# Where the running sum of the experts gets its scaled residual, and which places hold the weights of the second pair

## What is computed

```python
def grouped_moe(h, router_w, router_bias, w_gate, w_up, w_down):
    ...
    a = jnp.einsum('td,edf->etf', t, w_gate)
    u = jnp.einsum('td,edf->etf', t, w_up)
    hidden = jax.nn.silu(a) * u * gates.T.astype(t.dtype)[..., None]
    out = jnp.einsum('etf,efd->td', hidden, w_down)
    ...
    for l in range(DEPTH):
        ...
        x = layer_norm(ALPHA * x + mix, ln1_g[l], ln1_b[l])
        ffn = grouped_moe(x, router_w, router_bias, w_gate[l], w_up[l], w_down[l])
        x = layer_norm(ALPHA * x + ffn, ln2_g[l], ln2_b[l])
```

## Time and profile before

| | us |
|---|---|
| median of 3 runs | 1938.81 (1935.81 to 1940.58) |
| the profiled execution | 1934.94 |
| its span on the core | 1933.2 |
| TensorE busy | 1876.1 (97%) |
| DVE busy | 775.4 (40%) |
| DMA moved | 539.60 MB, mean 279 GB/s |

### The profile page before, as it was taken

How to read it: one execution, slowest core, us unless ns; L and a number is a source line. 1 busy time by engine, 2 the same in 40 slices (tenths; PEclk the granted TensorE clock), 3 DMA queues, 4 the chain that set the end, 5 groups by cost and what they waited for, 6 DMA issues and landing times.

```text
span 1933.2 us, 30131 instructions
## 1 busy us (share of the span) xinstructions
PE 1876.1 (97%) x12621; PEld 1218.6 (63%) x12621; DVE 775.4 (40%) x1463; ACT 298.1 (15%) x609; POOL 401.0 (21%) x406
## 2 busy tenths in 40 slices
PE   8999999999999999999999999999999999999996
PEld 7999988656644444444389989886565444444442
DVE  5657546643502111011486655566424021111015
ACT  1104210110211101111111141210102111111111
POOL 4467671012000000000005667710220000000001
PEclk9999999999999999999999999999999999999999
DMA  7444442228999999999944434421399999999997
GB/s 250 154 131 132 148 158 67 88 70 347 372 406 399 421 425 414 429 428 423 393 152 155 141 122 153 153 67 67 102 382 367 412 411 421 426 417 428 429 422 282
DMA packets 124649, 539.60 MB, mean 279 GB/s; under 512 B 14704, under 2 KB 19312, under 8 KB 85360
## 3 DMA queue, kind: packets, MB, share of 16 engines
q1 hardware_dynamic: 124528, 537.86, 71.2%
HBM read 535.73 MB, written 2.10 MB: 278 GB/s over the span
## 4 chain that ended last, share of the span: by engine, by line
PE 85%; DVE 8%; DMA 5%; issue 1%; ACT 1%; SPq 0%; DVEq 0%; ACTq 0%
PE bank L1539 20%; PE bank L1000 14%; PE bank L1005 10%; PE bank L1584 9%; PE bank L942 7%; PE bank L1425 6%; PE bank L1036 3%; DMA region_b<-in_w_up_dram 3%; PE bank L1276 3%; DMA x_t<-in_w_down_dram 2%; PE bank L1481 2%; PE bank L886 1%; PE bank L1437 1%; PE bank L1439 1%; DVE bank L2139 1%
## 5 line engine op out<-in xcount | busy, mean ns | idle before, releaser
L653 POOL TENSOR_TENSOR ring<-ring 128x512 f32<-128x512 f32 x72 | 95.5, 1327 | 1009.1 <-PE bank L1005 670.2
L2545 DVE TENSOR_TENSOR region_a<-bank,region_a 128x512 f32<-128x512 f32 x16 | 17.1, 1067 | 543.4 <-PE bank L1539 543.4
L1584 PE MATMUL bank<-ring,region_a 128*64 128x512 f32 x496 | 150.1, 602 | 0.6 <-DMA x_t<-in_w_down_dram 0.6
L1000 PE MATMUL bank<-x_t,ring 128*128 128x128 f32 x1152 | 147.6, 277 | 0.0
L1425 PEld LDWEIGHTS bank<-prob_t,x_nat 128*128 128x128 f32 x1024 | 117.9, 192 | 38.0 <-issue 37.3
L1000 PEld LDWEIGHTS bank<-x_t,ring 128*128 128x128 f32 x1152 | 137.0, 192 | 5.8 <-issue 5.7
L1425 PE MATMUL bank<-prob_t,x_nat 128*128 128x128 f32 x1024 | 127.1, 280 | 0.0
L1005 PE MATMUL bank<-ring,x_t 128*128 128x256 f32 x512 | 124.4, 381 | 0.0
L1539 PE MATMUL bank<-ring,region_a 128*64 128x512 f32 x368 | 121.7, 595 | 0.4 <-DMA x_t<-in_w_up_dram 0.4
L2561 DVE SCALAR_TENSOR_TENSOR y_lo<-bank,slot_gate,y_hi 128x512 fp32r<-128x512 f32 x64 | 48.1, 751 | 175.9 <-ACT y_hi L1843 171.5
L942 PE MATMUL bank<-ring,mix_acc 128*128 128x512 f32 x256 | 115.8, 595 | 0.0
(11 more groups left out here) (447 smaller groups left out, 3045.5 us busy)
## 6 DMA issues: line engine op xcount, KB each, us to landing
ring<-in_w_in_dram SPq DMA_DIRECT2D x80, 1024.0 KB, 5.0
ring<-in_w_down_dram SPq DMA_DIRECT2D x38, 1024.0 KB, 13.6
ring<-in_w_down_dram SPq DMA_DIRECT2D x18, 2048.0 KB, 13.6
ring<-in_w_gate_dram SPq DMA_DIRECT2D x34, 1024.0 KB, 9.6
ring<-in_w_out_dram SPq DMA_DIRECT2D x32, 1024.0 KB, 5.1
ring<-in_w_up_dram SPq DMA_DIRECT2D x24, 1024.0 KB, 13.1
region_b<-in_w_up_dram SPq DMA_DIRECT2D x24, 1024.0 KB, 14.6
region_b<-in_w_gate_dram SPq DMA_DIRECT2D x12, 2048.0 KB, 17.6
```

Source lines behind the costliest of these rows:

```text
L653: pool.tensor_tensor(t1, b12, b11, ALU.subtract).then_inc(combined_ready.sem, 1)
L1000: mm = pe.matmul(o[:, cols], rhs[:, a, cols], lhs[:, a, :], start=begins and b == 0, stop=ends, skip_group_check=True)
L1584: m = pe.matmul(bank[4 + c][rows, :], hid_t[:, f, rows], weights(n + e)[:, c * PANEL:(c + 1) * PANEL], start=(f == 0), stop=(f == FC - 1))
```

## The change

Three edits. The sum's buffer is filled with `ALPHA * x` in pair 0, after the picking matrix of pair 1 (`begin_sum`, eight instructions in each layer), and pair 1 adds to it as all others do. The two places in `mix_acc` are no longer usable for pieces of pair 1, since the sum now stands there earlier. The counter of DVE's steps grows by eight.

```diff
     for g in range(LEAD + FIRST, LEAD_PIECES):
         late = g >= LEAD_PIECES - EXP_SLOTS
-        usable = [home for home in range(LEAD + FIRST) if 3 * late <= home < LEAD or (LEAD <= home < LEAD + 2 and g < PAIR_PIECES + 16 and lead_last[home] < PAIR_PIECES)]
+        usable = [home for home in range(LEAD + FIRST) if 3 * late <= home < LEAD]
         LEAD_HOME[g] = min(usable, key=lambda home: lead_last[home])
...
-        dve_steps = signal("dve_steps", 388)
+        dve_steps = signal("dve_steps", 396)
...
-                def add_scattered(i, begin=False):
+                def add_scattered(i):
...
-                        got = bank[SCATTER_BANKS[n]][:, :]
-                        if begin:
+                        tt(a, bank[SCATTER_BANKS[n]][:, :], a, ALU.add).then_inc(scat_added.sem, 1)
+
+                def begin_sum():
+
+                    for t in range(NT):
+                        for c in range(4):
                             q0 = c * PANEL // KC
                             x = x_nat[:, t, :].rearrange("p (c q) -> p q c", c=KC)[:, q0:q0 + PANEL // KC, :]
-                            m = stt(out=a.rearrange("p (q c) -> p q c", c=KC), in0=x, scalar=ALPHA,
-                                    in1=got.rearrange("p (q c) -> p q c", c=KC), op0=ALU.mult, op1=ALU.add)
-                        else:
-                            m = tt(a, got, a, ALU.add)
-                        m.then_inc(scat_added.sem, 1)
+                            a = acc[:, t, c * PANEL:(c + 1) * PANEL].rearrange("p (q c) -> p q c", c=KC)
+                            s.do(ts(a, x, ALPHA, None, ALU.mult))
+                    s.sync()
...
-                        add_scattered(q, begin=second)
+                        add_scattered(q)
 
                     pick_pair(pair * 2 + 2).then_inc(pick2_ready.sem, 1)
+                    if first:
+                        begin_sum()
```

More of the change, by code:

```diff
@@ L2540, in column_stats, with pair_turn @@
                         s.do(dve.bn_stats(stats[:, t, c, :], bank[4 * t + c][:, :]))
-                def pair_turn(pair, q, first=False, second=False, last=False):
+                def pair_turn(pair, q, first=False, last=False):
                     dve.wait_ge(gateup_done.sem, q * 2 + 2)
@@ L2566, in _ @@
                 pair_turn(0, pairs0, first=True)
-                pair_turn(1, dve.snap(pairs0 + 1) if l else 1, second=True)
+                pair_turn(1, dve.snap(pairs0 + 1) if l else 1)
                 with dve.Fori(2, last_of) as pair:
```

## The result

The changed kernel takes 1953.8 us in the median of 4 runs (1952.70 to 1954.21), against 1938.44 us (1935.81 to 1940.58, 4 runs) before: a ratio of 1.0079, 95% interval 1.0065 to 1.0094. It is slower by 15.4 us; 16 were forecast.

What follows compares the result with a forecast made beforehand. Each expert stage was taken as bound by TensorE at its start and the weight stream at its end; lateness of 8.1 and 9.9 us, partly recovered, made 16 us on the 1938.81 median: 1954.8 us, range 1946 to 1962.

Steps and rivals of the forecast that it cites:

- Part 1: DVE in pair 1: plain addition shortens the pair by at most 3.49 us in layer 0, 1.78 in layer 1.
- Part 2: DVE in pair 0: begin_sum takes 7.75 us, ends at 553.4, before y_lo starts at 558.92, so costs nothing.
- doesn't fit under its cover: Rival: begin_sum overruns in pair 0, or pair 1 stays as long; pair 3 up to 5.3 us later, 1960.1 us; 3 in 100.
- Part 3: Pair 1's pieces 31 and 32 without mix_acc: stream later by about one piece, forgotten when the queue runs dry; price nothing.
- Part 4: Pair 4's second transfer waits for pair 3's end: 8.1 and 9.9 us late, 16 us in all including part 1's gain.
- the rival to this effect: TensorE pays only its own 3.7 us wait per layer and the stream catches up: +2.1, 1940.9 us; 6 in 100.
- One of the signs: Expected in the changed kernel's trace: pairs 4, 5 and 6 at 58.8 us or a little over.
- The sum: Both layers' lateness at the end, with part 1's gain included: 15.1 to 18.0 us, taken as 16 us.
- my upper end of 18.0: Lateness of both layers together if none of the transfer time lost in pair 4 comes back: 18.0 us.
- The clock rival: TensorE's clock falls after each layer's last wait, 1.7 us each, up to 3.4 us more, 1958.2 us; 4 in 100.

Runs made afterwards that it cites:

- the swap: Kernel before, only pieces 94 and 95 moved to the fourth place of region_b and the first of ring; 1957.81 us, ratio 1.0096.
- the table alone: Kernel before with only the changed line of the table, sum still begun in pair 1's scatter; 1959.11 us, ratio 1.0113.
- the passage is mended: Changed kernel, last 11 pieces of pair 3 kept off the first six places, so three transfers for pair 4 go out before pair 3 ends; 1941.01 us.
- sum five times over: Changed kernel with the eight instructions that begin the sum made five times over in pair 0; 1954.47 us, ratio 1.0084.

## Why the prediction was right, step by step

**Part 1, pair 1 shorter by 3.49 and 1.78 us.** Right within 0.02 us: pair 1 takes 54.72 and 54.71 us. The wait for DVE and the slow stretch behind it are both gone.

**Part 2, the sum in pair 0 for nothing.** The result is right, its two numbers are not. Eight instructions take 4.20 us; I had taken 7.75 and given 4.88 as the lower bound. And the cover doesn't end at 558.92, where `y_lo` starts, but at the scatter of pair 1, which is the first to read `y_lo`: the run with 21.37 us of it shows no loss. With this the rival "doesn't fit under its cover", from 13.3 us on, falls as a mechanism.

**Part 3, pieces 31 and 32 for nothing.** This step held only because of the next one. The first issue without `mix_acc` lands at 550.61 + 4.8 = 555.4 us; before, the piece was issued at 540.77 and landed after 10.2 us, at 551.0. The stream is 4.4 us late from here (in layer 1 by 4.6: 1518.45 + 4.9 against 1499.57 + 10.0, of a stage that starts 9.15 us later). In the changed kernel the queue that runs dry at the end of pair 3 makes this forgotten, as I had written: with the swap, which keeps the two places, the time is that of the table alone within the noise. Where the passage is mended no later dry stretch is there, and of these 9 us in both layers 3.5 reach the end against the kernel before, and 7.1 against the one that has both the places and the cheap scatter. So the price is nothing beside part 4, and not nothing without it.

**Part 4, the second transfer for pair 4.** Right in layer 0, and for the end of both stages. For layer 0 I had a landing at 732.3 (7.4 us after an issue at the end of pair 3) and 3.7 us of TensorE's wait; the trace has 732.50 and 3.93. For layer 1 I had taken the same 7.4 us, and it was 8.93, with a wait of 5.44 us. This is no accident of one execution: in the kernels table only, two pieces swapped and sum five times over it was 8.95, 8.84 and 8.79 us in layer 1. Why was not settled. The two transfers issued behind it land after 15.6 us (15.3 in layer 0), so the stream as a whole is hardly later for it. At the end of the stages the last transfer for which TensorE waits is late by 880.67 - 872.88 = 7.8 us in layer 0, where 6.5 to 8.1 stood, and by 19.0 - 9.15 = 9.8 us in layer 1 (1908.00 against 1889.03, from a stage that starts at 1476.39 instead of 1467.24), where 8.6 to 9.9 stood. The stream did not catch up: the rival to this effect would have ended at 1940.9 us.

One of the signs was wrong: pair 4 at 58.8 us or a little over. It takes 64.9 us in layer 0 (725.08 to 789.98) and 65.1 in layer 1 (1692.92 to 1758.02). TensorE loses all of its lead in this one pair, in layer 0 by waits of 3.93 and 2.55 us and by 16 matmuls at a lower clock. Pairs 5 and 6 take 58.7 and 59.9 us in layer 0, 59.6 and 57.9 in layer 1, near what was forecast.

**The sum.** The profiled executions differ by 19.0 us, a little over my upper end of 18.0: 7.8 and 9.8 in the stages, and 1.35 us between the last wait of layer 0 and the expert stage of layer 1. The last is not the change's: this stretch took 594.36 us before (872.88 to 1467.24) and 595.72 in the changed kernel, but 594.39 (881.66 to 1476.05) with the sum five times over, which has the change too. The medians differ by 15.4, and that this is so near to 16 is in part luck. The profiled execution before is one of its quickest, as I had written, and the changed kernel's runs lie close together; between 15 and 19 us the figure depends on which executions are compared.

**The clock rival.** It had been priced by a wait for DVE. The new waits for a load, 3.93 and 5.44 us, did bring slow stretches: 16 matmuls take 6.33 and 6.35 us behind them instead of 3.58 (granted clock 0.94 from 728 to 784 us), 2.75 us each and not 1.7. They are hidden, since TensorE soon waits for the stream again. The rival spoke of the last wait of each layer, and there nothing is new. In layer 0 a slow stretch follows it in both kernels, 32 matmuls in 8.79 us instead of 7.09, before and after:

```profile
873.01 8.79 PE L1539 MATMUL bank<-region_b,prob_t 128*64 128x512 f32 x32 [2.69 <-DMA region_b<-in_w_up_dram]
```

```profile
880.80 8.79 PE L1539 MATMUL bank<-region_b,prob_t 128*64 128x512 f32 x32 [2.71 <-DMA region_b<-in_w_up_dram]
```

In layer 1 it follows in neither (16 matmuls in 3.65 us in both).

## What to carry to other kernels

When a table of buffers is changed at one end, look at who sits where at the other: the two buffers given up cost nothing here that the runs could tell (and 3.5 to 7 us only once the passage was mended), and the new residents of two places, some 60 pieces later, cost nearly all. Where a stream of transfers sets the end, look for the issue that has to wait for the end of a unit of work: when that wait ends, enough of what was issued ahead of it must still be in flight to last until its own transfer lands. An estimate from the rows of this case, 7.4 us to land and 4.9 us for each transfer of 2 MB, is one and a half transfers. Of the kernels here, two issued ahead left a short dry stretch and three left none; zero and one ahead cost a full transfer more for each that was missing, in each layer, and the stream never made it up. Time saved on the engine that runs ahead counts where the stream waits for that engine: in the changed kernel through the end of pair 3, and in the kernel that begins the sum early in pair 1 to some 3.6 us.

## What the runs showed that I had not expected

An instruction of DVE with the permuted read of `x_nat` takes 0.53 us for 128x512 as a multiplication out of SBUF (40 in 21.37 us) and 0.97 us when it also adds a block from PSUM (eight in 7.75), although a plain addition of such a block takes 0.61. Which operand makes the difference was not tried.

A wait of nearly one length was followed by a slow stretch of TensorE in one place and not in another: before, 1.79 us in layer 0 was, and the pair took 58.22 us; in layer 1 the pair took 56.51, with a wait of 1.76 us. With the table alone, layer 1's wait of 1.77 us was followed by one as well (granted clock 0.67 from 1572 to 1576 us), and the pair took 1588.51 - 1530.27 = 58.24 us.

The kernel before has a spread of 8.3 us over 19 runs beside one set of experiments (1933.25 to 1941.53), the changed kernel one of 1.5 us over 4. Why it spreads was not settled.
